# A hybrid attention layer on one core: the mixer's SBUF region starts at another remainder

## The reference, cut to what matters

```python
def reference(x, ...):
    y = token_mixer(x, ...)                      # four branches A, B, C, D of 8 heads x 64
    x = layer_norm(DEEPNORM_ALPHA * x + y, ln1_g, ln1_b)
    y = conv_glu_ffn(x, ...)                     # 1024 -> 2816 (twice) -> 1024
    return layer_norm(DEEPNORM_ALPHA * x + y, ln2_g, ln2_b)

    # in token_mixer
    proj = einsum('bsnk,nkd->bsnd', branches, w_branch)
    gates = sigmoid(x @ w_gate + b_gate)
    merged = sum(gates * proj, axis=2)
    return merged @ w_out

    # in conv_glu_ffn
    a = x @ w_up
    a = conv_b + sum(conv_w[j] * ap[:, j:j + L] for j in range(3))   # ap: a, padded by two tokens in front
    return (gelu(a) * (x @ w_ffn_gate)) @ w_down
```

## Time and profile before

| | |
|---|---|
| median of 3 runs | 2306.04 us (2301.39 to 2308.06) |
| the profiled execution | 2308.06 us |
| its span, first to last instruction | 2306.3 us |
| TensorE (PE) busy | 2164.5 us, 94% |
| VectorE (DVE) busy | 1448.9 us, 63% |
| ScalarE (ACT) busy | 935.4 us |
| GpSimd (POOL) busy | 780.0 us |
| mean granted TensorE clock | 0.983 |

### The profile page before, as it was taken

How to read it: one execution, slowest core, us unless ns; L and a number is a source line. 1 busy time by engine, 2 the same in 40 slices (tenths; PEclk the granted TensorE clock), 3 DMA queues, 4 the chain that set the end, 5 groups by cost and what they waited for, 6 DMA issues and landing times. The chain is left out here.

```text
span 2306.3 us, 28237 instructions
## 1 busy us (share of the span) xinstructions
PE 2164.5 (94%) x10600; PEld 1794.6 (78%) x10600; DVE 1448.9 (63%) x2389; ACT 935.4 (41%) x1621; POOL 780.0 (34%) x598
## 2 busy tenths in 40 slices
PE   7989988999899989999999999998999999999996
PEld 5778877778777777888788878787777777788775
DVE  2878778876888766622466651467666666654643
ACT  2555654125641266621355551324333333333331
POOL 2123232212322223222222323415555555634343
PEclk9999999999999999999999999999999999999998
DMA  3121000121011100011211112222322222174332
GB/s 115 39 22 29 19 24 19 42 55 28 15 42 42 50 10 14 10 46 51 71 31 46 42 37 74 87 110 75 99 83 82 76 75 78 56 247 168 123 119 110
DMA packets 177768, 147.68 MB, mean 64 GB/s; under 512 B 23768, under 2 KB 155864, under 8 KB 177632
## 3 DMA queue, kind: packets, MB, share of 16 engines
q1 hardware_dynamic: 176880, 143.74, 20.5%
q10 hardware_dynamic: 752, 2.13, 0.3%
HBM read 125.89 MB, written 19.96 MB: 63 GB/s over the span
## 5 line engine op out<-in xcount | busy, mean ns | idle before, releaser
L1549 POOL TENSOR_TENSOR w_lo<-w_raw,w_hi 128x1024 fp32r<-128x1024 f32 (+1 forms) x102 | 215.7, 2115 | 588.7 <-ACT w_hi L1151 588.4
L629 PE MATMUL pair<-act_hi,w_hi 128*128 128x512 f32 x704 | 280.2, 398 | 7.7 <-DVE act_lo L1932 5.6
L629 PE MATMUL pair<-act_lo,w_hi 128*128 128x512 f32 x704 | 276.1, 392 | 0.0
L629 PE MATMUL pair<-act_hi,w_lo 128*128 128x512 f32 x704 | 275.9, 392 | 0.0
L1151 ACT ACTIVATE w_hi<-w_raw 128x1024 fp32r<-128x1024 f32 (+1 forms) x102 | 94.0, 922 | 372.4 <-PE pair L629 354.5
L1860 DVE TENSOR_TENSOR pt_lo<-chunk,pt_hi 128x512 fp32r<-128x512 f32 (+1 forms) x272 | 173.5, 639 | 79.7 <-ACT pt_hi L1179 76.6
L1179 ACT ACTIVATE pt_hi<-chunk 128x512 fp32r<-128x512 f32 (+1 forms) x272 | 150.5, 553 | 165.0 <-PE chunk L722 163.1
L1591 POOL TENSOR_SCALAR prob<-prob,att 128x256 f32<-128x256 f32 (+4 forms) x172 | 117.3, 692 | 282.8 <-DVE att L1804 282.8
L629 PE MATMUL pair<-heads,w_hi 128*128 128x512 f32 x512 | 160.8, 395 | 11.6 <-DVE mid L2130 6.6
L645 PE MATMUL pair<-act_hi,w_hi 128*128 128x512 f32 x384 | 166.2, 433 | 0.0
L629 PEld LDWEIGHTS pair<-act_hi,w_hi 128*128 128x128 f32 x704 | 133.8, 190 | 35.8 <-DVE act_lo L1932 6.4
(11 more groups left out here) (288 smaller groups left out, 5253.4 us busy)
## 6 DMA issues: line engine op xcount, KB each, us to landing
dn_raw<-in_w_down SPq DMA_DIRECT2D x44, 512.0 KB, 4.0
w_raw<-in_w_in SPq DMA_DIRECT2D x37, 512.0 KB, 3.8
w_raw<-in_w_gate SPq DMA_DIRECT2D x32, 512.0 KB, 4.0
up_raw<-in_w_up SPq DMA_DIRECT2D x22, 512.0 KB, 4.1
gate_raw<-in_w_ffn_gate SPq DMA_DIRECT2D x22, 512.0 KB, 5.3
hidden<-gelu_s SPq DMA_DIRECT2D x22, 512.0 KB, 2.9
h_in<-hidden SPq DMA_DIRECT2D x44, 256.0 KB, 4.3
mid<-in_x SPq DMA_DIRECT2D x16, 512.0 KB, 7.1
```

The source lines that it names most:

```text
L629: last = nc.tensor.matmul(dst[0:cols, s:s + HALF], w[:, k, :], a[:, k, s:s + HALF], start=(k == 0 and n == 0), stop=(k == kt - 1 and n == 2))
L1549: nc.gpsimd.tensor_tensor(split_into(1, g), w_raw[:, g % 2, 0:kt * cols], split_into(0, g).bitcast(F32), ALU.subtract).then_inc(lo_ready, 1)
```

## The change

The address at which the mixer region begins is worked out in another way. Before, it is the first byte from the end of the first region on that is congruent to `act_at` modulo 512; after, it is the first multiple of 128. The line after it, unchanged, sizes the filler from the result.

```diff
@@ -269,7 +269,7 @@
         stat = sb("stat", [P, 64])
         att = sb("att", [P, 24])
 
-        mixer_at = act_at - (act_at - nc.sbuf_base) // 512 * 512
+        mixer_at = -(-nc.sbuf_base // 128) * 128
         sb("to_boundary", [P, (mixer_at - nc.sbuf_base) // 4])
         mixer = ExitStack()
         heads = sb("heads", [P, 8, SEQ], F32R, mixer)
```

## The result

The changed kernel takes 2321.87 us (median of 4 runs, 2320.67 to 2323.20) where the kernel before takes 2306.34 (4 runs, 2301.39 to 2308.06). The ratio is 1.007, 95% interval 1.0053 to 1.0089: 0.7% slower, 15.5 us. The forecast was no measurable change, with 0.19 on slower. The median lies 0.13 us inside the upper end of the stated range, but the kernel did get slower by more than the noise, so the forecast itself is wrong.

The account below looks back on a forecast made before the run. The prediction took TensorE, busy 94% of the span, to bound the kernel. Its terms, 0 + 0 + 0 - 0 to 1 us, gave 2306.0 us on the runs' median (2308 on the profiled execution), range 2292 to 2322.

Parts of the forecast that it names:

- 0.19 on slower: Whole kernel: chance of being slower by over 0.3%, 0.15 through TensorE plus 0.04 through the vector side.
- What bounds the kernel: Whole span: TensorE, busy 94%, sets the time; its 512-column matmuls follow each other every 226.7 ns.
- the 13.3 ns between matmuls: TensorE: 226.7 ns spacing less 213.3 ns for 512 columns; the only slack in the bound an address could reach.
- TensorE, "I take 0": 4056 matmuls joining the regions: no change from unequal phase, bounds 54 us either way.
- slower by TensorE: Rival, matmuls joining the regions: out-of-phase operands delay each other, 13.5 us more, 2320; chance 0.15.
- 0.63 us a block: Up stage: TensorE idle per block, 19.67 us apart less 19.04 of products; x 21 = 13 us.
- VectorE, ScalarE, GpSimd, 0: Operations joining the regions and VectorE-GpSimd delays: no change; delay bounds 19 us either way.
- the four medians that it named as signs: VectorE and GpSimd: gelu_s 1225, t_sum 682, w_sum<-gate_raw 1786 and dn_lo 2405 ns should stand.
- The two rivals on this side: VectorE-GpSimd delays on the path: grow by half of 19 us, 2316, chance 0.04; or shrink, 2296, chance 0.07.
- DMA, 0 to -1 us: Loads into the mixer region (up_raw, gate_raw, dn_raw): hidden, so 0, at best -1 us.
- The argument for "same": Whole kernel: no effect of a size that can be measured, within 0.3%, 2306; chance 0.66.

Follow-up runs that it names:

- e1: Kernel before with both regions starting at a multiple of 512 (remainder 0): 2306.72 us, ratio 1.0003.
- e4: Kernel before with the mixer region 256 bytes above the congruent place: 2304.27 us, ratio 0.9995.
- e2: Kernel before with w_hi, w_lo and the small constants behind them 128 bytes further up, mixer region unmoved: 2318.37 us, ratio 1.006.
- e8: Kernel before with the mixer region 128 bytes above the congruent place: 2319.06 us, one execution.
- e9: Kernel before with the feed-forward views alone 128 bytes further up, out of phase: 2314.96 us, ratio 1.0032.
- e11: Kernel before with the convolution's second tap made on the first 64 tokens alone: 2289.66 us, one execution.
- e12: Changed kernel with the convolution's second tap made on the first 64 tokens alone: 2313.07 us, one execution.
- e3: Changed kernel with the feed-forward views 128 bytes further up, back in phase: 2311.95 us, ratio 1.0039 against the kernel before.
- e7: Kernel before with the mixer region 64 bytes above the congruent place: 2315.36 us, one execution.
- e10: Kernel before with the mixer region 96 bytes below the congruent place: 2324.45 us, one execution.

## Why the prediction was wrong, point by point

**What bounds the kernel: right.** TensorE's spacing did set the time, and the 13.3 ns between matmuls was the place that an address reached: they became 19 to 20.

**TensorE, "I take 0": this step failed.** Its reason was that the 13.3 ns were the same for all pairs, whatever the distance of the tiles, and that a conflict of addresses would show a spread. But all the distances in that trace are multiples of 512, so in the one respect that counts the pairs were one pair. The text said itself that the rows do not show an unequal phase, and then drew on them all the same. Nor was the spacing the same "wherever one looks": L645 had 231.3 ns in that very trace, which I had not looked at. What the runs showed: 0 at a difference that is a multiple of 256 (e1, e4), 4.9 to 5.9 ns at 128 (after, e2, e8, e9), but for L645 with 1.1 (e2).

**The rival "slower by TensorE" was the mechanism.** It priced the matmul at a quarter of 13.3 ns, 3.3, and gave 2320. Measured: 4.9 to 5.8 ns, 22.9 us gross, 15.5 net. That its 2320 came near is luck, for two errors cancel: the price was too low, and nothing was taken off for stages in which TensorE waits anyway.

**What is absorbed.** The prediction put the idle time of TensorE at 0.63 us a block, and e11 bears that out: 19.67 less 19.04. After the change it is 19.96 (1870.34 to 1890.30) less 19.52, 0.44. The chain over the convolution, gelu and first_s still took nearly its time (its first tap a little less, as above), and TensorE came to it later. I had counted this wait only as something that could grow or shrink, not as cover for a slower TensorE. e11 and e12 show it.

The stages' differences, after minus before, are 7.2 us up to the output projection, 1.4 in it, 4.4 in up and 3.1 in down. In the last three that is 8.9 of a gross 18.5, so 9.6 us are hidden there. The first stretch works the other way: 7.2 where the products out of heads explain 4.4. Most of the rest goes with the clock. By the clock records TensorE had the lower of its two levels for 51.2 us of this stretch before and for 58.0 after. At half the speed, my estimate is that the 6.8 us more cost up to half of that, 3.4. It was 30.7 us in e4, whose stretch ends 9.9 us sooner than that of the kernel before (1476.5 against 1486.4), and again 51.2 in e1, which ends at 1487.8. Whether the change has a part in this is not shown. One execution of each was profiled, and e11, the same kernel as before up to there, had 41.0.

**VectorE, ScalarE, GpSimd, 0: right for the four medians that it named as signs.** 1225 became 1226, 682 became 680, 1786 became 1784, 2405 became 2404. The two rivals on this side fall as causes. But the delays of VectorE did not all stand, as the `w_sum` rows above show. With the feed-forward views back in phase (e3) the two are at 998 and 1295 again and the first tap at 1664; with these alone out of phase (e9) they are at 893, 1126 and 1601. The first tap is short (1584 to 1601) in every run with the whole tap whose up stage has 232 ns or more, and long (1652 to 1664) in the others. That it follows the slower TensorE, because VectorE then meets GpSimd's work at another moment, fits this and was not tested.

**DMA, 0 to -1 us: right for the time.** The rule of the Trainium skill, page "DMA: Bandwidth & Descriptors", section "How a descriptor splits into AXI transactions", has transactions start at multiples of 256 bytes, so that a piece that starts elsewhere takes more of them; the page tells of what a transaction reads, and these loads write into SBUF. The traces agree in the sign for two of the three loads: up_raw lands in 3.9 to 4.0 us where its address is such a multiple (after, e1, e8, e9) and in 4.1 to 4.2 where it isn't (before, e2 to e7, e10), gate_raw in 5.0 to 5.1 against 5.3 to 5.5. That is about a twentieth, not a fifth. dn_raw stays at 3.9 to 4.0 in all of them. No wait depends on it.

**The range and chances.** The 0.19 on slower was too small. The argument for "same" rested on rows that could not speak on the question.

## What to carry to other kernels

Where TensorE sets the time and its matmuls are 512 columns of fp32 (F32R in this kernel; no other type was tried), look at the addresses of weights and moving operand modulo 256: equal ones cost 227 ns in most of this kernel, others up to 234. A region that only happens to be in phase with another is a fact that the kernel rests on, and a cleaner-looking alignment can undo it. When a trace has only one value of a quantity, a spread of zero in it says nothing about other values: keep the bound, and give it a chance that fits. And a slower engine costs less than count times price wherever it was waiting already; here about two thirds of it.

## What the runs showed of the hardware

The distance between two matmuls of 512 fp32 columns depends on the two SBUF addresses that they read: the weights' minus the moving operand's, modulo 256 bytes. The order counts: with the weights 64 bytes below 229 ns, with them 64 bytes above 233.4. At a remainder of zero it is 227, in either region and at region starts that leave 0, 128 or 384 on division by 512, but for L645, which has 231.3 at zero and 232.4 at 128 (e2). Transposes of 128 columns whose operands join the regions did not change (116.9 and 116.1 ns). Which of the two reads is held up, and whether a matmul meets the load of its own weights or of the next one's, no run here tells: within a stage all tiles had one phase. Steps finer than 32 bytes were not tried.
